# Three RMS norms whose row scale is multiplied in behind the products, in a two-model fp32 kernel

## The reference, cut to what matters

```python
def rmsnorm(x, g):
    y = x * lax.rsqrt(jnp.mean(x * x, axis=-1, keepdims=True) + EPS)
    return y * g

def conv_ffn(h, w_up, conv_w, conv_b, w_down):
    u, g = jnp.split(h @ w_up, 2, axis=-1)
    g = causal_dwconv(g, conv_w, conv_b)      # over rows: w0*g[t-2] + w1*g[t-1] + w2*g[t] + b
    return (jax.nn.silu(g) * u) @ w_down

for l in range(2):
    h = rmsnorm(x, norm_mix_g[l])
    mix_out = ...   # layer 0: mLSTM; layer 1: band attention on q = h @ b_w_in and on k_pad, v_pad
    x = x + jnp.concatenate([mix_out, mem_out], axis=-1) @ w_out
    x = x + conv_ffn(rmsnorm(x, norm_ffn_g[l]), w_up, conv_w, conv_b, w_down)
    if l == 0:
        k_pad, v_pad = split(rmsnorm(x, kv_norm_g) @ w_kv)
x = rmsnorm(x, final_g)
```

## Time and profile before

| | us |
|---|---|
| median of 3 runs | 1751.65 (1751.22 to 1752.39) |
| the profiled execution | 1753.42 |
| its span, first to last instruction | 1751.6 |
| PE busy | 1604.5 (92%) |
| DVE busy | 1003.1 (57%) |
| ACT busy | 691.8 (39%) |
| mean granted clock of TensorE, of full speed | 0.946 |

### The profile page before, as it was taken

How to read it: one execution, slowest core, us unless ns; L and a number is a source line. 1 busy time by engine, 2 the same in 40 slices (tenths; PEclk the granted TensorE clock), 3 DMA queues, 4 the chain that set the end, 5 groups by cost and what they waited for, 6 DMA issues and landing times. The chain is left out here.

```text
span 1751.6 us, 29166 instructions
## 1 busy us (share of the span) xinstructions
PE 1604.5 (92%) x12106; PEld 1471.6 (84%) x12106; DVE 1003.1 (57%) x1404; ACT 691.8 (39%) x820; POOL 18.3 (1%) x40
## 2 busy tenths in 40 slices
PE   6979889999799889999679989899999989889997
PEld 6876689999777689999467766867999989889997
DVE  5574656666643366666644554444766666666665
ACT  5343433434343444344433542233443443343432
POOL 0000000000200000000000000000000000000000
PEclk9997999999899999999789987899999999999999
DMA  5331635445534735545114454502344534435451
GB/s 223 127 120 72 235 126 193 176 184 192 127 145 183 274 122 192 190 178 206 42 54 164 193 192 163 190 21 97 145 177 182 190 130 162 158 119 204 171 188 49
DMA packets 39490, 273.90 MB, mean 156 GB/s; under 512 B 4784, under 2 KB 5936, under 8 KB 6768
## 3 DMA queue, kind: packets, MB, share of 16 engines
q1 hardware_dynamic: 37296, 264.26, 40.7%
q0 software_dynamic: 1392, 5.77, 1.4%
q10 hardware_dynamic: 720, 2.68, 0.4%
HBM read 271.64 MB, written 1.05 MB: 156 GB/s over the span
## 5 line engine op out<-in xcount | busy, mean ns | idle before, releaser
L1417 PE MATMUL L<-h_hi,whi 128*128 128x256 f32 (+1 forms) x2096 | 623.7, 298 | 55.2 <-DVE h_lo L849 17.8
L1417 PE MATMUL L<-h_lo,whi 128*128 128x256 f32 (+1 forms) x2096 | 617.4, 295 | 0.0
L1417 PE MATMUL L<-h_hi,wlo 128*128 128x256 f32 (+1 forms) x2096 | 617.1, 294 | 0.0
L1417 PEld LDWEIGHTS L<-h_hi,whi 128*128 128x128 f32 x2096 | 416.8, 199 | 72.6 <-issue 66.6
L1417 PEld LDWEIGHTS L<-h_lo,whi 128*128 128x128 f32 x2096 | 416.9, 199 | 3.8
L1417 PEld LDWEIGHTS L<-h_hi,wlo 128*128 128x128 f32 x2096 | 415.8, 198 | 4.2
L800 DVE TENSOR_TENSOR wlo<-raw,whi 128x2048 fp32r<-128x2048 f32 x107 | 244.9, 2290 | 138.3 <-ACT whi L445 138.1
L919 DVE TENSOR_TENSOR wlo<-raw,whi 128x2048 fp32r<-128x2048 f32 x96 | 219.8, 2290 | 115.3 <-ACT whi L545 115.3
L445 ACT ACTIVATE whi<-raw 128x2048 fp32r<-128x2048 f32 x107 | 202.5, 1902 | 62.3 <-PE L L1417 34.4
L1417 PE MATMUL D<-hd_hi,whi 128*128 128x256 f32 x704 | 199.7, 284 | 6.4 <-DVE hd_lo L940 6.4
L1417 PE MATMUL D<-hd_hi,wlo 128*128 128x256 f32 x704 | 199.4, 283 | 0.0
(11 more groups left out here) (253 smaller groups left out, 1959.6 us busy)
## 6 DMA issues: line engine op xcount, KB each, us to landing
raw<-in_units SPq DMA_DIRECT2D x251, 1024.0 KB, 4.8
arena<-in_relx POOLq DMA_DIRECT2D x12, 128.0 KB, 4.0
arena<-in_nax POOLq DMA_DIRECT2D x1, 1536.0 KB, 6.7
t<-in_mem ACTq DMA_DIRECT2D x1, 1024.0 KB, 7.8
x<-in_x ACTq DMA_DIRECT2D x1, 1024.0 KB, 12.3
arena<-in_ctx POOLq DMA_DIRECT2D x1, 1024.0 KB, 5.0
out<-t SPq DMA_DIRECT2D x8, 128.0 KB, 2.0
arena<-in_relx POOLq DMA_DIRECT2D x12, 64.0 KB, 4.1
```

Of the source, the lines that this page charges most:

```text
L1417: ins = mm(dst, w[a], h[b], start=start and n == 0, stop=stop and n == 2, skip_group_check=True)
```

## The change

Three norms are changed: that behind `a_out`, that behind `ffn0` (both gains) and that behind `b_out`. `h_hi` and `h_lo` are now made of `x * g` without `rs`: ACT's `rows_hi` (activation Identity with the gain as scale) rounds straight from `x`, pair by pair, right after it squares that pair, and DVE's `rows_lo` makes `x * g - h_hi` in one instruction for each block, placed one evacuation behind. `t` isn't written there any more.

PE does the sums of the last two pairs (behind `a_out` and `b_out`), or all four (behind `ffn0`), inside the first job, behind its sixth block. DVE's statistics and ACT's root come after one more weight unit.

`rs` is multiplied in where products leave PSUM: bank g_i into a new tile `f_g` ahead of each convolution (both FFNs, 11 times each), the four banks D at the end of each FFN into `f_g` or `f_y` ahead of the addition to `x`, keys, queries and memory queries in their own evacuation (a second operand of it), values by `rs_col`, where the rows are in the partitions: two tiny matmuls turn `rs` and DVE copies the two columns. The bank u_i isn't scaled, since the factor of `u` is that of the whole product, and comes with D.

```diff
+            def rows_hi(g, i, col=0):
+                for c in (2 * i, 2 * i + 1):
+                    A.activation(h_hi[:, c, col:col + T], x[:, c, :], ACT.Identity, scale=g(c)) \
+                        .then_inc(R["h_hi_done"], 1)
...
-            jobs("a_out", lambda n, j: square(x, n))
+            def a_rows(n, j):
+                square(x, n)
+                rows_hi(lambda k: vc("ffn_g", k), n)
+            jobs("a_out", a_rows)
+            upto(JOBS["ffn0"][2].unit)
             root()
-            apply()
             ffn("ffn0", 0, ACT.Silu)
-            stat(x, ffn_parts(0))
-            apply(before=finished("ffn0"))
-            apply(col=T)
+            for i in range(4):
+                act.wait_ge(R["x_ready"], i + 1)
+                square(x, i)
+                rows_hi(lambda k: vc("kv_g", k), i)
+            for i in range(4):
+                rows_hi(lambda k: vc("mix_g", KB + k), i, T)
+            upto(JOBS["kv_v0"][0].unit)
+            root()
             jobs("kv_k0")
             jobs("b_qm")
...
+            def rows_lo(g, i, col=0):
+                for c in (2 * i, 2 * i + 1):
+                    dve.wait_ge(R["h_hi_done"], rounded[0] + c + 1)
+                    V.scalar_tensor_tensor(h_lo[:, c, col:col + T], x[:, c, :], g(c), h_hi[:, c, col:col + T].bitcast(FP),
+                                           ALU.mult, ALU.subtract).then_inc(R["h_lo_done"], 1)
+                if i == 3:
+                    rounded[0] += KB
+            def over_rows(ap):
+                return ap.unsqueeze(1).to_broadcast([P, 2, T])
...
-            def residual(name, gate=None):
+            def residual(name, gate=None, g=None):
+                def rows(n):
+                    dve.wait_ge(job_evac, JOBS[name][n].banked + 1)
+                    rows_lo(g, n)
...
-                jobs(name, evac)
-            def ffn(name, f, offsets, gate=None):
+                jobs(name, evac, {} if g is None else {n: (lambda n=n: rows(n - 1)) for n in range(1, 4)})
+                if g is not None:
+                    rows(3)
+            def ffn(name, f, offsets, gate=None, scaled=True, g=None):
...
-                    conv(f_y, pair(g_bank[:]), [tap(i, n) for n in range(3)], tap(i, 3), offsets) \
-                        .then_inc(job_evac, 1)
+                    if scaled:
+                        conv(f_y, pair(g_bank[:]), [tap(i, n) for n in range(3)], tap(i, 3), offsets) \
+                            .then_inc(job_evac, 1)
+                    else:
+                        step(V.tensor_tensor(f_g, pair(g_bank[:]), over_rows(rs[:]), ALU.mult))
+                        sync()
+                        conv(f_y, f_g, [tap(i, n) for n in range(3)], tap(i, 3), offsets).then_inc(job_evac, 1)
...
+                if not scaled:
+                    stat()
+                    dve.wait_ge(R["rs_done"], stats[0])
...
-                        V.tensor_tensor(dst, dst, pair(Dn[n][:]), ALU.add).then_inc(R["x_ready"], 1)
+                        part = f_y if n % 2 else f_g
+                        step(V.tensor_tensor(part, pair(Dn[n][:]), over_rows(rs[:]), ALU.mult))
+                        sync()
+                        V.tensor_tensor(dst, dst, part, ALU.add).then_inc(R["x_ready"], 1)
+                        if g is not None and n:
+                            dve.wait_ge(R["x_ready"], 4 * f + n)
+                            rows_lo(g, n - 1)
...
+                if g is not None:
+                    dve.wait_ge(R["x_ready"], 4 * f + 4)
+                    rows_lo(g, 3)
...
-            residual("a_out")
+            residual("a_out", g=lambda k: vc("ffn_g", k))
+            ffn("ffn0", 0, CAUSAL3, scaled=False, g=lambda k: vc("kv_g", k))
+            for i in range(4):
+                rows_lo(lambda k: vc("mix_g", KB + k), i, T)
+            upto(JOBS["kv_v0"][0].unit)
             stat()
-            apply(lambda k: vc("ffn_g", k))
-            ffn("ffn0", 0, CAUSAL3)
-            stat()
-            apply(lambda k: vc("kv_g", k), before=finished("ffn0"))
-            apply(lambda k: vc("mix_g", KB + k), col=T)
+            dve.wait_ge(R["rs_done"], stats[0])
             def store_k(n):
-                return lambda b: V.tensor_copy(bk[:, 2 * n:2 * n + 2, :], pair(b[:]))
+                return lambda b: V.tensor_tensor(bk[:, 2 * n:2 * n + 2, :], pair(b[:]), over_rows(rs[:]), ALU.mult)
             def store_v(n):
-                return lambda b: V.tensor_copy(bv[:, :, 256 * n:256 * n + 256], pair(b[:]))
+                def run(b):
+                    step(V.tensor_scalar(bv[:, 0, 256 * n:256 * n + 256], b[:, 0:T], rs_col[:, 0:1], None, ALU.mult))
+                    return V.tensor_scalar(bv[:, 1, 256 * n:256 * n + 256], b[:, T:512], rs_col[:, 1:2], None, ALU.mult)
+                return run
             def store_q(n):
-                return lambda b: V.tensor_scalar(bq[:, 2 * n:2 * n + 2, :], pair(b[:]), 0.125, None, ALU.mult)
+                return lambda b: V.scalar_tensor_tensor(bq[:, 2 * n:2 * n + 2, :], pair(b[:]), 0.125, over_rows(rs[:]),
+                                                        ALU.mult, ALU.mult)
...
-            jobs("b_qm", lambda n, j, b: V.tensor_scalar(bqm, pair(b[:]), 0.125, None, ALU.mult))
+            jobs("b_qm", lambda n, j, b: V.scalar_tensor_tensor(bqm, pair(b[:]), 0.125, over_rows(rs[:]), ALU.mult, ALU.mult))
+            dve.wait_ge(R["rs_turn"], 1)
+            step(V.tensor_copy(rs_col[:], Dn[2][:, 0:2]))
+            sync()
...
-            residual("b_out")
-            stat()
-            apply(lambda k: vc("ffn_g", KB + k))
-            ffn("ffn1", 1, CAUSAL3)
+            residual("b_out", g=lambda k: vc("ffn_g", KB + k))
+            ffn("ffn1", 1, CAUSAL3, scaled=False)
...
+                        if mid and n == 5:
+                            mid()
...
+            def last_sums():
+                sums(2)
+                sums(3)
+            def residual(name, mixed, order=range(KB), late=False):
                 if name == "e_out":
                     pe.wait_ge(R["mix_lo_done"], MIX["na"])
                 jobs(name, after={1: lambda: sums(0), 2: lambda: sums(1)}, mixed=mixed, order=order)
-                sums(2)
-                sums(3)
+                if not late:
+                    last_sums()
...
-            residual("a_out", lambda k: MIX["memA"] + (k // 3 + 1 if k < 6 else 0), [6, 7, 0, 1, 2, 3, 4, 5])
-            ffn("ffn0", 0)
-            jobs("kv_k0", fresh=True)
+            residual("a_out", lambda k: MIX["memA"] + (k // 3 + 1 if k < 6 else 0), [6, 7, 0, 1, 2, 3, 4, 5], late=True)
+            ffn("ffn0", 0, last_sums, sums_behind=False)
+            jobs("kv_k0", fresh=True, mid=stat)
             jobs("b_qm", fresh=True)
+            pe.wait_ge(R["rs_done"], stats[0])
+            for tb in range(2):
+                ins = mm(Dn[2][:, tb:tb + 1], rs[0:1, tb * P:tb * P + P], ones[0:1, 0:1], start=True, stop=True)
+            ins.then_inc(R["rs_turn"], 1)
             attention(T_B, len(T_A), 2, MIX["ml"], NARROW, BESIDE_B)
             turn(23)
-            residual("b_out", lambda k: MIX["memB"] + (k + 1 if k < 6 else 0), [6, 7, 0, 1, 2, 3, 4, 5])
-            ffn("ffn1", 1)
+            residual("b_out", lambda k: MIX["memB"] + (k + 1 if k < 6 else 0), [6, 7, 0, 1, 2, 3, 4, 5], late=True)
+            ffn("ffn1", 1, last_sums)
```

More of the change, by code:

```diff
@@ L189, in build @@
         sc = sb("sc", [P, KB, 2])
+        rs_col = sb("rs_col", [P, 2])
         mod = sb("mod", [P, 2, 48, 2])
@@ L248, in build @@
         f_h = area(9728, 2, T)
+        f_g = area(10240, 2, T)
         bk = area(2048, 6, T)
@@ L672, in _, with b_rows @@
             upto(JOBS["b_out"][0].unit + 1)
-            jobs("b_out", lambda n, j: square(x, n))
+            def b_rows(n, j):
+                square(x, n)
+                rows_hi(lambda k: vc("ffn_g", KB + k), n)
+            jobs("b_out", b_rows)
+            upto(JOBS["ffn1"][2].unit)
             root()
-            apply()
             ffn("ffn1", 1, ACT.Silu)
@@ L953, in ffn @@
                 n0 = steps[0]
-                per = 5
+                per = 5 if scaled else 6
                 with dve.Fori(2, NI - 1) as i:
@@ L1418, in mm3, with job @@
                 return ins
-            def job(j, first=False, h_base=None, mixed=None, parts=(0, 1), order=range(KB)):
+            def job(j, first=False, h_base=None, mixed=None, parts=(0, 1), order=range(KB), mid=None):
                 s = j.unit % RING
@@ L1465, in job, with jobs @@
                     ins.then_inc(job_done, 1)
-            def jobs(name, fresh=False, after={}, mixed=None, order=range(KB)):
+            def jobs(name, fresh=False, after={}, mixed=None, order=range(KB), mid=None):
                 for n, j in enumerate(JOBS[name]):
-                    job(j, n == 0 and (fresh or mixed is not None), h_in[0] if fresh else None, mixed, order=order)
```

(11 more changed lines are left out.)

8 lines of the change are left out of this document (4 added, 4 removed).

## The result

| | before | changed |
|---|---|---|
| median, us | 1751.43 (4 runs, 1750.88 to 1752.39) | 1729.62 (4 runs, 1728.54 to 1731.43) |
| the profiled execution | 1753.42 | 1731.43 |
| its span | 1751.6 | 1729.6 |

The ratio is 0.9876, with a 95% interval of 0.9859 to 0.9893: 21.8 us less, where 18.4 were forecast. The predicted 1733.3 is 3.7 us too high and its range, 1728.5 to 1740, holds the result.

A forecast was written before the change was run, and what follows sets the result against it. PE, busy 92% of the span, was taken as the bound, through its waits and lower clock. Gains 7.6 + 7.6 + 5.0 - 1.8 = 18.4 us gave 1733.3 from 1751.65, range 1728.5 to 1740.

The forecast's parts named there:

- The heads of the FFNs: Behind a_out and b_out: first job ends 8.2 us earlier, less a 0.6 wait for g2; gain 7.6 each.
- The multiply: Bank g times rs ahead of each convolution: 0.68 us, bounded by 0.42 and 1.1.
- The loop: FFN loops: 22 convolutions each 0.45 us longer, hidden by ACT's 3.84 wait for PE; cost zero, 10 us without that cover.
- The norm behind `ffn0`: From ffn0 to the attention's first tile: start at 463.4 instead of 468.43, gain 5.0 us, bounds 3 to 6.
- Behind `ffn1`: Final norm keeps its form, but the evacuation of D lengthens the path to it: loss 1.8 us (1.2 to 3).
- The head takes half back: Rival, FFN heads: slower multiply, unhurried taps and a lower-clock stretch cost 7.8 us, so 1741; 12%.
- Short waits take PE's clock in `kv_k0` and `b_qm`: Rival, behind ffn0: 96 matmuls at 1.2 GHz cost 9 us more, 4.3 of it lost, so 1737.6; 8%.
- A slow broadcast operand: Rival: multiply slow at twelve places on the path; at the reciprocal's rate 34 us more, so 1767; 2%.
- The `ffn0` norm gives nothing: Rival, behind ffn0: its chain grows where the forecast took the lower end, so 1738; 6%.
- The band's bias: Attention: starts one root later, landing at 475 against the mask at 486.5; eleven us of cover, no cost.

The follow-up runs named there:

- `b_qm` first: Changed kernel with DVE evacuating b_qm and copying rs_col ahead of the wlo of b_q0's unit, not behind it: 1728.01 us, ratio 0.9867; again 1728.30, 0.9863.

## Why the prediction was right, and where it was off

**The heads of the FFNs** were forecast at 7.6 each and gave 7.60 and 7.46, by the forecast's own path: the job starts where `a_out` ends and waits for no `h_lo`, the sums fit inside it, the multiply comes at 248.48 (forecast 249.95, less the 1.3 by which this execution was ahead). Two small misses cancel: down0 came 7.87 and 7.75 earlier, not 8.2, because the eight records of the sums took 1.5 us and not 1.4 and the job's other products slightly longer; and g2 is late by 0.2 to 0.3, not 0.6 (the forecast's own 271.35 and 270.9 give 0.45). The doubled multiply shows that the chain to g2, which the forecast said has no slack, has indeed none: two multiplies of 0.69 more, one ahead of it and one in it, cost 1.44.

**The multiply** was taken as 0.68, from its nearest row, and is 0.69; the first tap from SBUF was taken as 0.41, from a row of another stage, and is 0.41. The bounds of 0.42 and 1.1 weren't needed.

**The loop** costs nothing, as forecast, even with two multiplies.

**The norm behind `ffn0`** gave 5.66 for 5.0, and the same instruction ends last. The term was a little too large in its ACT part: `wlo` of `kv_v0` starts 16.66 us behind the last unit, where 453.4 - 436.36 = 17.04 was forecast, and the instructions behind it overlap a little more. The wait of nearly 5 us is 2.94, partly because PE reaches it later: the sums of all four pairs stand in its own job. The clock fell once, behind that wait, to 0.57 over 453 to 461, as forecast; keeping `b_qm`'s evacuation ahead of `wlo` removes wait and drop, and is worth 5.8 us in the stage.

**Behind `ffn1`** the forecast was 1.8 lost, and the table has 0.68 gained. This is the step that failed in size: it followed DVE's chain alone to the fourth addition, and the addition did come 1.84 later, but PE's sums stood in the same place and had been the later of the two. Up to the first statistics the true loss is 0.97, shown by the kernel without that multiply. The other 1.65 are clock: the context's statistics come 2.74 us sooner behind the first ones because their sums ran at 1.00 and not at 0.57, as the row of before shows, and the last ones come 1.08 later.

```profile
834.90:841.50 6.60, 6.46 (x16) 4.92 (x16) 3.24 (x11) 1.54 (x3) 0.00 (x0) 0.57 0.00 0
```

Two profiles of one kernel differ by 2.3 in this stage, so the 1.65 can't be credited to the change. It isn't shown that they have nothing to do with it either: over all profiles the stage takes 37.92 to 40.21 us in the six with the multiply and no added matmuls, four of them at 37.9 to 38.0, and 37.37 to 38.98 in the five without it, four of them at 38.7 to 39.0.

**The sum.** With 0.97 for the last term, the change itself is worth 7.6 + 7.5 + 5.7 - 1.0 = 19.8 us in the profile; 18.4 were forecast. The remaining 2.2 of the 22.0 are 1.3 ahead of `a_out`'s end, 0.4 in the attention, 1.65 behind `ffn1` and -1.1 in the second model, none of it at a place where a gain was forecast. PE's code is the same in all four, though the evacuations in the attention have the factor now. Whether the medians hold the same 2.2 can't be told: there are profiles of single executions only. The result lies inside the range only by its extension: the bounds of the terms gave a gain of at most 21.5, so 1730, and the step to 1728.5 was meant for a faster convolution and shorter lower-clock stretches in the heads, neither of which is what came. That part is luck.

**The rivals.** *The head takes half back*: not seen, the clock is at 1.00 from 239 to 264. *Short waits take PE's clock in `kv_k0` and `b_qm`*: the series of short waits that the trace of before lacked is there now, three of 0.37 to 0.47 between groups of twelve products, and the clock over 434 to 442 is 1.00. What the Trainium skill describes ("TensorE: Matmul & The Clock Gate", section "A second HAM failure mode: psum-queue depth-cycling"), a clock that swings with many small idles between groups of matmuls, did not come about with these three. *A slow broadcast operand*: the factor is read once for each of the two halves of 256 columns, and the multiply costs what one with two plain operands costs (680), 684 to 693 ns for 512 columns. *The `ffn0` norm gives nothing*: it gave most of what its bounds allowed. *The band's bias*: its loads have landed 8 to 10 us ahead of the mask, less than the 11 forecast but enough.

What stays open: `b_qm` first gains 5.5 to 5.8 us in its stage in two profiles and 2.0 to 2.3 in the medians beside and across the changed kernel's. Part of the difference in each profile is where the lower clock fell in other stages, but what the unprofiled runs did isn't known. Only their mean granted clock is: 0.952 to 0.954 in the four runs of `b_qm` first, 0.953 or 0.954 in the changed kernel's beside them. So it didn't rise, though the drop behind the wait is gone in the profiles; that the lower clock fell elsewhere instead would fit this, but no run tests it.

## What to carry to other kernels

A norm's row scale commutes with the product, and where the norm stands as a serial chain over three engines between two products, moving it behind the next product removes the wait and also the slow stretch that PE pays after it, here 5.3 and 2.5 us at each of two places. Cost the multiply where it lands: in a loop whose engines wait for PE it is free, in the head ahead of the loop each us is a us. Before pricing a longer step at a join, look for the other engine that ends there: a chain that is second to it by 0.9 us can grow by 0.9 for nothing. And where an experiment clears one stage, read the others too: the gain of a stage and that of the whole kernel differed by 1.5 to 3.5 us here.

## What the runs showed of the hardware

**Keeping PE at work in a wait paid although no wait ended sooner by it.** In the waits of 3.3, 9.9 and 4.5 us behind `ffn1` matmuls on ones kept the clock at 1.00, and 5.7 us were gained in the stages that they touch. Too many of them cost what they give (fourteen against nine behind `a_out`: 0.42 us each).

**A small wait left standing doesn't cost the clock**: 0.39 ahead of `ffn0`, 0.37 to 0.47 three times in `kv_k0`, 1.60 ahead of each last unit, and 0.34 ahead of the first tile, all with 1.00 behind them. Those of 2.65 to 5.08 behind `a_out`, `b_out`, `ffn0` and `ffn1`, ahead of a product, had 0.50 to 0.66 in the first 4 us behind them (ahead of those of 2.65 to 2.94 PE did only two matmuls of one column in 0.6 us). The one of 3.27 ahead of the context's sums had 1.00 in some executions and not in others.

**Unchanged code varies by 4 us.** In the eight profiles of kernels whose code is the same up to there, the end of `a_out` lies between 238.01 and 242.45, and the stretches at the lower clock are not the same ones: in the latest, 210 to 220 is at 0.74, and in the earliest it is at 1.00. A gain of 2 us in one profile says little unless it is read at the stage that the edit touches.
